# Scores, transposes and values of the chunked attention placed over 14 of a unit's 16 weight chunks

## What is computed

```
h = rmsnorm(x, norm_g)
aq, ak, av, ag, bq, bk, bv, bg = split(h @ w_in)
A: 16 heads of 64; softmax(q k / 8 + relbias[head, clip(i - j)]) v over the own chunk of 64 and 8 before it
B: 16 query heads, 2 key heads; rotary q, k; window of two chunks; a sink logit per head
x = x + concat(A * silu(ag), B * silu(bg)) @ w_out
```

## Time and profile before

| | us |
|---|---|
| median of 3 runs | 1624.63 (1624.28 to 1625.23) |
| span of the profiled execution | 1622.9 |
| TensorE busy | 1612.2 (99%) |
| VectorE busy | 1126.2 (69%) |
| ScalarE busy | 879.3 (54%) |
| GpSimd busy | 100.2 (6%) |
| 16 units of mixer A | 51.2 each |

### The profile page before, as it was taken

One profiled execution on the slowest core, in us unless ns is written; L12 is line 12 of the kernel. 1 busy time (PEld: TensorE's weight loads), 2 busy tenths in 40 slices (PEclk: granted clock), 3 DMA queues, 4 the chain that ended last, 5 costly groups with the idle time before them and its releaser, 6 DMA issues.

```text
span 1622.9 us, 24332 instructions
## 1 busy us (share of the span) xinstructions
PE 1612.2 (99%) x8249; PEld 1372.5 (85%) x8249; DVE 1126.2 (69%) x2563; ACT 879.3 (54%) x1911; POOL 100.2 (6%) x74
## 2 busy tenths in 40 slices
PE   9999999999999999999999999999999999999997
PEld 8888888888888888899988888888888888888997
DVE  7666665566577877888855665666567677788875
ACT  7555555555646666433455555555546466654333
POOL 0000000000121200010000000000002211000000
PEclk9999999999999999999999999999999999999999
DMA  7232222231322322344442232222232323223443
GB/s 253 90 102 104 77 90 90 90 115 58 120 94 91 97 106 91 103 152 155 162 142 79 90 112 93 85 83 90 93 112 74 115 91 100 96 91 117 130 143 117
DMA packets 50014, 174.30 MB, mean 107 GB/s; under 512 B 6496, under 2 KB 10880, under 8 KB 35984
## 3 DMA queue, kind: packets, MB, share of 16 engines
q1 hardware_dynamic: 49472, 172.69, 31.4%
q10 hardware_dynamic: 432, 0.55, 0.1%
q0 software_dynamic: 32, 0.08, 0.0%
HBM read 160.10 MB, written 8.47 MB: 104 GB/s over the span
## 4 chain that ended last, share of the span: by engine, by line
PE 97%; DVE 2%; DMA 1%; issue 0%; SPq 0%; ACT 0%; DVEq 0%
PE ps_proj L605 23%; PE ps_proj L604 23%; PE ps_proj L603 23%; PE ps_t L660 2%; PE ps_o L673 2%; PE ps_s L651 1%; PE ps_s L652 1%; PE ps_o L715 1%; PE ps_s L690 1%; PE ps_o L603 1%; PE ps_o L605 1%; PE ps_o L604 1%; PE ps_t L701 1%; PE ps_o L831 1%; PE ps_proj L831 1%; PE ps_o L827 1%
## 5 line engine op out<-in xcount | busy, mean ns | idle before, releaser
L603 PE MATMUL ps_proj<-act_hi,w_hi 128*128 128x512 f32 x1632 | 642.2, 394 | 0.0
L605 PE MATMUL ps_proj<-act_hi,w_lo 128*128 128x512 f32 x1632 | 638.1, 391 | 0.0
L604 PE MATMUL ps_proj<-act_lo,w_hi 128*128 128x512 f32 x1632 | 637.2, 390 | 0.0
L1313 DVE TENSOR_TENSOR w_lo<-w_raw,w_hi 128x512 fp32r<-128x512 f32 (+1 forms) x528 | 382.7, 740 | 128.7 <-ACT w_hi L925 124.8
L925 ACT ACTIVATE w_hi<-w_raw 128x512 fp32r<-128x512 f32 (+1 forms) x528 | 336.6, 656 | 181.4 <-DVE w_raw L1627 58.3
L605 PEld LDWEIGHTS ps_proj<-act_hi,w_lo 128*128 128x128 f32 x1632 | 306.3, 188 | 66.0
L603 PEld LDWEIGHTS ps_proj<-act_hi,w_hi 128*128 128x128 f32 x1632 | 306.7, 188 | 58.3
L604 PEld LDWEIGHTS ps_proj<-act_lo,w_hi 128*128 128x128 f32 x1632 | 306.8, 188 | 57.8
L925 ACT ACTIVATE probs<-probs,rden 128x128 f32<-128x128 f32 (+3 forms) x128 | 72.1, 563 | 119.2 <-DVE rden L1406 119.2
L991 ACT ACTIVATE probs<-probs,nmax 128x128 f32<-128x128 f32 (+3 forms) x128 | 71.9, 562 | 93.9 <-DVE nmax L1385 90.9
L1313 DVE TENSOR_TENSOR arena<-ps_t,arena 128x512 fp32r<-128x512 f32 (+4 forms) x168 | 85.1, 510 | 43.4 <-ACT arena L925 42.6
(11 more groups left out here) (294 smaller groups left out, 2287.2 us busy)
## 6 DMA issues: line engine op xcount, KB each, us to landing
w_raw<-w SPq DMA_DIRECT2D x107, 1024.0 KB, 4.8
w_raw<-w SPq DMA_DIRECT2D x98, 256.0 KB, 3.6
temp<-temp SPq DMA_DIRECT2D x72, 64.0 KB, 4.1
strips_tables<-ext SPq DMA_DIRECT2D x16, 256.0 KB, 5.8
temp<-xT SPq DMA_DIRECT2D x16, 256.0 KB, 4.2
xs<-xy SPq DMA_DIRECT2D x16, 256.0 KB, 4.3
temp<-xs SPq DMA_DIRECT2D x16, 256.0 KB, 4.0
strips_tables<-ext SPq DMA_DIRECT2D x16, 224.0 KB, 5.7
```

Source lines behind the costliest of these rows:

```text
L603: pe.matmul(dst, wh, act_hi[:, k, :], start=start, stop=False)
L604: pe.matmul(dst, wh, act_lo[:, k, :], start=False, stop=False)
L605: return pe.matmul(dst, wl, act_hi[:, k, :], start=False, stop=stop)
L1313: return nc.vector.tensor_tensor(dst, src, hi, ALU.subtract)
```

## The change

Scores stand at steps 0, 1, 3, 4, 6, 7, 9, 10, transposes two steps after each (2, 3, 5, 6, 8, 9, 11, 12), values at 7 and 13. In the loop units hi_q moves from p = 8 to 10 and lo_q from 8 to 11, in the last unit hi_k from 8 to 11 and lo_k from 9 to 11, and VectorE waits for its own key rests before the take of the third tile, which writes the same buffer (t_k). The same instructions run as before.

```diff
-PV_A = (6, 11)
-TURN_A = tuple(range(2, 2 + E_A))
+SCORES_A = (0, 1, 3, 4, 6, 7, 9, 10)
+TURN_A = tuple(p + 2 for p in SCORES_A)
+PV_A = (7, 13)
...
-                if p < E_A:
-                    scores_a(g, v, e0, p)
+                if p in SCORES_A:
+                    scores_a(g, v, e0, SCORES_A.index(p))
...
             def duties(T, L, p, nxt):
                 kind, g = nxt
                 if kind in ("a", "a_first"):
-                    if p == (8 if kind == "a" else 12):
+                    if p == (10 if kind == "a" else 12):
                         hi_q(lambda: act.wait_ge(proj_free, T + 2), g)
                     if p == 13:
                         hi_k(lambda: act.wait_ge(proj_free, T + 3))
                 if kind == "b":
-                    if p == 8:
+                    if p == 11:
                         hi_k(lambda: act.wait_ge(rope_done, L * ROPES + 1))
...
                 if kind == "a":
                     if p == 8:
                         take(T, 1, t_q)
+                    if p == 11:
                         lo_q(g)
...
-                    if p == 9:
+                    if p == 11:
                         lo_k(L * V_LAYER + PAIRS)
                     if p == 12:
+                        dve.wait_ge(k_done, L * V_LAYER + V_LAYER)
                         take(T, 2, t_k)
```

More of the change, by code:

```diff
@@ L1036, in attend @@
                     half_out(g, PV_A.index(p))
-                if p < E_A:
-                    softmax_a(e0, p, other)
+                if p in SCORES_A:
+                    softmax_a(e0, SCORES_A.index(p), other)
                 else:
@@ L1490, in attend @@
                 g, v, e0 = att
-                if p < E_A:
-                    bias_a(v, L * PAIRS + ab, e0, p)
+                if p in SCORES_A:
+                    bias_a(v, L * PAIRS + ab, e0, SCORES_A.index(p))
                 if p in TURN_A:
@@ L1500, in attend @@
                 other()
-                if p < E_A:
-                    invert(e0, p)
+                if p in SCORES_A:
+                    invert(e0, SCORES_A.index(p))
             def attend_b(L, point):
```

## The result

The changed kernel takes 1638.71 us (median of 4 runs, 1636.16 to 1639.85) against 1624.45 us (4 runs of before beside it, 1624.20 to 1625.23): a ratio of 1.0085, 95% interval 1.0071 to 1.0100. It is slower, as predicted, but by 14.3 us where 7.0 were predicted, and it lies 3.2 us above the upper end of the range. The profiled execution of after has a span of 1636.2 us, 13.3 us more than before's 1622.9.

The account below looks back on a forecast made before the run. The prediction took TensorE, without slack, to bound the kernel. Parted groups 1.4, last units 4.9 and loop units 0.7 sum to 7.0 us on a 1622.9 us span, 1629.9, hence a 1631.6 us median; range 1628.3 to 1635.5.

Parts of the forecast that it names:

- What bounds: TensorE, busy 1612.2 of 1622.9 us, has no wait in the units; late chains over ScalarE and VectorE decide.
- Part 1: Scores parted from transposes on TensorE, three pairs in each of 16 units at 0.03 us: 1.4 us, 1.0 to 1.9.
- Part 2: Second values in each layer's last unit late by 1.94 us plus 0.5 for a rotation: 4.9 us, 3.5 to 6.1.
- Part 3: Query work in the chain to the 14 loop units' second values: a tie, 0.7 us in all, 0 to 2.8.
- all loop units wait too: Hand-overs 0.15 us longer in sum make each of 14 loop units wait 0.2 us: 1633.7 us; chance 0.10.
- The clock rival: TensorE's granted clock halves for one chunk after each last-unit stall: 5.4 us more, 1637 us; chance 0.04.
- Not slower: The last units' chain fits in the single chunk, leaving only the parted groups: 1626.0 us, 0.1%; chance 0.10.
- faster: Spreading evens ScalarE and VectorE and removes TensorE waits in units; under 0.1 us per group could shrink; chance 0.02.

Follow-up runs that it names:

- e3: The changed kernel with the last units' hi_k, lo_k and the loop units' hi_q, lo_q all moved to p = 12: 1626.64 us, ratio 1.0015.
- e2: The changed kernel with hi_q and lo_q of the loop units moved to p = 12, behind score 7's hi_p and lo_p: 1630.62 us, ratio 1.0042.
- e1: The changed kernel with the last unit's hi_k and lo_k moved from p = 11 to p = 12: 1632.80 us, ratio 1.0052.
- e6: The changed kernel with scores and transposes in pairs, values at p = 9 and 14, their turn at p = 3, key copies at p = 10, lo_p before biases: 1621.94 us.
- e5: The changed kernel with the second rotation's second and third GpSimd operations on 8 of 512 columns, output partly unrotated: 1635.95 us, ratio 1.0069.
- e7: The changed kernel with the last units' key copies and rests cut into halves, eight instead of four each: 1639.49 us, ratio 1.0096.
- e9: The changed kernel with the last units' key copies and rests cut into halves and the loop units' hi_q, lo_q at p = 12: 1634.25 us, ratio 1.0061.

## Why the prediction was right and wrong

- **What bounds.** Right: TensorE had no slack, and most of the loss came as waits for a chain over the two other engines, ahead of the values that I named. The rest of the profiled 13.3 us are the parted groups (0.6) and the clock (1.6).
- **Part 1, parted groups.** 1.4 us predicted. e3's unit shows 0.04 us, so 0.6 us in all. That is under the lower bound of 1.0; I had priced all three pairs of a unit by one of them.
- **Part 2, the last units.** 4.9 us predicted; 5.6 us measured without the clock, or 3.0 us a layer without the wait that before had elsewhere. Both are inside its range. The steps: up to the normalisation 3.80 instead of 2.89 us, which is the rotation's 0.9 us where I took 0.5; normalisation to key copies 1.52, copies 2.58, rests 2.82, as read. Two small terms had the wrong sign or size. TensorE started 0.14 us after lo_p's end (459.49 + 0.69 to 460.32), not 0.03. And I gave a late release 0.11 us for free, while a TensorE that has waited takes 1.24 us from the first value to the next projection matmul instead of 1.16 (1267.44 to 1268.68 in after, 1248.79 to 1249.95 in before).
- **Part 3, the loop units: here the prediction failed.** The step is the sum "9.39 to 9.47 us, against the same 9.38", called a tie at 0.05 us a unit. Measured are 9.78 us for the chain against 9.45 us for TensorE (the last projection matmul before the values starts at 405.55, and 0.23 us later the values were due). The chain's surplus has three parts. First, the w_lo began 0.65 us after the lo_p of score 6 where I read 0.52. It waits for the chunk's w_hi, which ends at 402.47 + 0.63 = 403.10: this instruction stands on ScalarE behind the query copies and hi_p, I had left it out of the chain, and it began 0.52 us after hi_p. Where hi_p stands behind the normalisation, as in e2's unit (398.29 and 398.66), it begins 0.37 us after it; why it is later behind the copies no run shows. Second, from the w_lo to lo_q it is 0.73 instead of 0.61 to 0.69 us. Third, the hand-over to TensorE is again 0.15 instead of 0.03 us. The wait of 0.33 us and 0.09 us more for the first matmuls behind it (406.11 to 407.36, 1.25 us) make 0.42, and 0.04 for the parted groups make 0.46; measured are 0.44 us a unit. Without the parting it is 0.40 us a unit, 5.6 us in all (after against e2; by the times of e1 against e3, 1632.80 - 1626.64 = 6.2 us), where I had 0.7. That the query work makes these waits is shown by e2; the split of the 0.33 us into its parts is read from the one trace.
- **The rival "all loop units wait too"** was the true case, priced at 0.2 us a unit, half of what it costs. Its chance of 0.10 was too low: I had a difference of 0.01 to 0.09 us between two sums of some ten and five read terms, and took the errors as if they could not all point one way. Fourteen copies of one such tie are one bet, not fourteen.
- **The clock rival** (0.04) came true in part. It was priced at 2.7 us a fall; 1.6 us was measured, for the one fall in the profiled execution. By their times the four runs had none to two each. The only row at 0.50 that I had was the program's end, and I took from it that short waits are safe; no row had such a wait in it. Why the clock falls in one layer and not in the other stays open.
- **Not slower, faster:** fell, as expected. A loop unit of e3, which has no wait, lasts 51.23 us against before's 51.19, so the spread alone gave TensorE nothing.
- **The range** failed because two cases held together: its upper end had the loop waits at only 0.2 us a unit and no fall of the clock beside them. With both at what they cost, 7.0 + 14 x 0.35 + 1.6 would have been 13.5 us.

## What to carry to other kernels

Where work is moved so that a chain over two engines must end within a gap, compare the time from the last transposes to their use before and after, and don't count on a near tie: this sum of read terms was short by 0.31 to 0.39 us, and a wait that begins costs a slow start on top (0.09 us here), in every copy of the loop. Count in the chain everything that stands ahead on both engines, the chunk's own w_hi included. If work is to be regrouped on a full TensorE, try larger lots with two chunks left for the chain (e6, 2.7 us faster than before), rather than more and smaller ones (e3, 2.5 us slower).

## What the runs showed of the hardware

- **The clock falls at short waits, and not in each run.** After waits of 1.9 us (e5), 2.8 (after) and 3.4 (e7) TensorE's granted clock went from 1.00 to 0.50 for 3.4 us in one layer and not in the other, with the same instructions and nearly the same wait in both; in e9 for 6.8 us. Neither of e2's two waits of 2.7 us was followed by a fall. The fall cost 1.6 us in after and 2.7 us in e9. In after, e5 and e7 it came 0.1 to 1.1 us after TensorE had started again, in e9 while it still waited. The 0.2 to 0.3 us waits of the loop units and the waits of 1.2 to 1.3 us in e1 and e3 were never followed by one in a profile. The Trainium skill, TensorE: Matmul & The Clock Gate, section What's actually happening, has the gate watch activity in windows that run free of the kernel, so that the same kernel can differ from run to run. The traces agree in that the falls differ between equal places; what decides between the two layers of one execution no run here shows.
- **The lock between VectorE and GpSimd** showed again in places that a schedule had merely shifted: 1.59 us for a w_lo of 0.69 (after), 0.69 again with the rotation cut short (e5), and 3.37 for two of 1.29 together (e3). The Trainium skill, SBUF — State Buffer, section Who interferes with whom, calls it an exclusive lock on a shared port pair, and e5 agrees with that: alone, the same w_lo takes 0.69 us. In e3 the meeting is read from the trace alone.
- **TensorE's start after a wait** is 0.14 to 0.15 us behind the end of VectorE's instruction in after, and the seven value matmuls then take 0.08 to 0.09 us more than the 1.16 us without a wait (1.24 at 1267.44, 1.25 at 406.11).
